# Router products between output tiles, expert 0 gathered before the full sort, and a software-pipelined expert loop

## What is computed

```python
x1 = layer_norm(ALPHA * x + mixer(x))                  # mixer: attention + retention, then @ w_out
# hierarchical MoE: top-1 of 4 groups, then top-2 of its 8 experts, 32 experts in all
g_logits = x1 @ w_group_router + b_group_router        # 4
e_logits = x1 @ w_expert_router + b_expert_router      # 4 x 8
g_sel = argmax(g_logits); top2 = top_k(e_logits[g_sel], 2)
weights = softmax(g_logits)[g_sel] * softmax(top2)
for e in experts:                                      # the rows of each expert
    hid = silu(rows @ w_gate[e]) * (rows @ w_up[e])    # 2048 -> 512
    y = hid @ w_down[e]                                # 512 -> 2048
x2 = layer_norm(ALPHA * x1 + sum over the token's two experts of weight * y)
```

## Time and profile before

| | us |
|---|---|
| median of three runs | 2180.9 (2179.12 to 2181.01) |
| the profiled execution, its own time | 2180.76 |
| its span | 2179.0 |
| PE busy | 2017.9 (93%) |
| DVE busy | 958.5 (44%) |
| ACT busy | 591.8 (27%) |
| POOL busy | 44.2 (2%) |
| mean granted TensorE clock | 0.948 |
| DMA, mean over the span | 283 GB/s |

### The profile page before, as it was taken

How to read it: one execution, slowest core, us unless ns; L and a number is a source line. 1 busy time by engine, 2 the same in 40 slices (tenths; PEclk the granted TensorE clock), 3 DMA queues, 4 the chain that set the end, 5 groups by cost and what they waited for, 6 DMA issues and landing times.

```text
span 2179.0 us, 23608 instructions
## 1 busy us (share of the span) xinstructions
PE 2017.9 (93%) x9124; PEld 1264.4 (58%) x9124; DVE 958.5 (44%) x1258; ACT 591.8 (27%) x736; POOL 44.2 (2%) x59
## 2 busy tenths in 40 slices
PE   9999999999999999999977988889888888998885
PEld 7888888888888888888855533333333333333331
DVE  5444554544444545565545433322333333233335
ACT  4444444334444344453423200000000000000000
POOL 0000000000000000000000000000000000000000
PEclk9999999999999999999989999999999989998997
DMA  7565455465555544566682599999999999999994
GB/s 237 183 200 177 155 168 169 156 202 173 193 184 164 174 159 161 182 229 228 204 313 76 209 429 428 428 428 428 428 429 429 429 429 428 428 429 429 428 429 174
DMA packets 147427, 617.01 MB, mean 283 GB/s; under 512 B 21024, under 2 KB 21152, under 8 KB 122272
## 3 DMA queue, kind: packets, MB, share of 16 engines
q1 hardware_dynamic: 147360, 616.09, 73.7%
HBM read 613.95 MB, written 2.10 MB: 283 GB/s over the span
## 4 chain that ended last, share of the span: by engine, by line
issue 57%; PE 35%; DVE 5%; ACT 2%; DVEq 0%; POOL 0%; POOLq 0%
PE PS L850 20%; PE PS L869 13%; DVE Z L1601 3%; PE PS L887 1%; DVE SG L1571 1%; PE PS L840 1%; ACT TG L1105 1%; PE PS L858 1%; ACT HT L1107 1%; POOL RSTD L1645 0%; PE PS L802 0%; ACT ZH L1085 0%; POOLq L1644 0%; DVE HB L1573 0%; PE PS L792 0%
## 5 line engine op out<-in xcount | busy, mean ns | idle before, releaser
L464 DVE TENSOR_TENSOR WL<-RAW,WH 128x1024 fp32r<-128x1024 f32 x384 | 457.6, 1221 | 394.7 <-ACT WH L460 393.8
L475 PE MATMUL PS<-WH,XH 128*128 128x512 f32 x1216 | 485.7, 399 | 4.6 <-DVE WL L464 3.4
L477 PE MATMUL PS<-WH,XL 128*128 128x512 f32 x1216 | 475.4, 391 | 0.0
L476 PE MATMUL PS<-WL,XH 128*128 128x512 f32 x1216 | 474.4, 390 | 0.0
L460 ACT ACTIVATE WH<-RAW 128x1024 fp32r<-128x1024 f32 x384 | 394.3, 1057 | 277.0 <-PE PS L477 223.2
L850 PE MATMUL PS<-W,XE 128*64 128x512 f32 x1984 | 430.9, 592 | 0.0
L850 PEld LDWEIGHTS PS<-W,XE 128*64 128x64 f32 x1984 | 139.3, 137 | 286.4 <-issue 286.4
L869 PE MATMUL PS<-W,HT 128*64 128x512 f32 x1024 | 290.8, 732 | 15.2 <-ACT HT L1107 15.2
L475 PEld LDWEIGHTS PS<-WH,XH 128*128 128x128 f32 x1216 | 228.9, 188 | 54.7 <-DVE WL L464 8.6
L477 PEld LDWEIGHTS PS<-WH,XL 128*128 128x128 f32 x1216 | 228.6, 188 | 49.2
L476 PEld LDWEIGHTS PS<-WL,XH 128*128 128x128 f32 x1216 | 229.0, 188 | 45.3
(11 more groups left out here) (262 smaller groups left out, 1360.8 us busy)
## 6 DMA issues: line engine op xcount, KB each, us to landing
RAW<-in_w_in_dram SPq DMA_DIRECT2D x304, 512.0 KB, 4.5
W<-in_w_expert_gate_dram SPq DMA_DIRECT2D x64, 2048.0 KB, 12.6
W<-in_w_expert_up_dram SPq DMA_DIRECT2D x64, 2048.0 KB, 17.0
W<-in_w_expert_down_dram SPq DMA_DIRECT2D x64, 2048.0 KB, 12.6
RAW<-in_w_branch_ret_dram SPq DMA_DIRECT2D x32, 512.0 KB, 4.8
RAW<-in_w_out_dram SPq DMA_DIRECT2D x32, 512.0 KB, 5.1
RAW<-in_w_branch_attn_dram SPq DMA_DIRECT2D x16, 512.0 KB, 4.6
XN<-in_x_dram SPq DMA_DIRECT2D x4, 512.0 KB, 8.2
```

Source lines behind the costliest of these rows:

```text
L464: dve.tensor_tensor(WL[:, i % RING], RAW[:, i % RING], WH[:, i % RING].bitcast(F32), ALU.subtract).then_inc(lo_done, 1)
L475: pe.matmul(PS[:, bank + t], hs, wh, start=first and j == 0, stop=False)
L476: pe.matmul(PS[:, bank + t], hs, wl, start=False, stop=False)
L477: mm = pe.matmul(PS[:, bank + t], ls, wh, start=False, stop=end)
```

## The change

Parts, in order of time:

1. **Router weights.** Loaded in the branch stage behind tiles 3 to 9, as 11 DMAs (runs of 64 and 128 bytes in the place of 16 and 32); DVE multiplies them by the norm's scale and bias behind branch tiles 18 to 23. The loads behind output tile 11 are gone but for RC.
2. **Logits from raw residual chunks.** Behind output tiles 10, 18 and 26 PE turns a chunk of un-normalised Z (8 turns), ACT copies it two tiles later, and behind tiles 14, 22 and 30 PE multiplies it by the weights (8 products 36 wide). The last chunk follows the last tile. Normalisation is put on the logits: LOG = logits * rstd + (NMR * column sums + bias).
3. **Norm and scaling.** ACT alone normalises Z and writes its high parts, reordered; POOL forms the low part of token tile 0, scales S1B and B1B, multiplies and adds them into Z (4 passes of 128x2048), clears the XT pad. DVE's four scaling passes are gone.
4. **Expert 0 first.** DVE builds SEL for the first 64 places, PE gathers 64 columns for 16 k (64 products 64 wide), ACT writes XE, `gate_up(0)` follows in one piece; the full sort of all 512 places comes after it.
5. **The expert loop** is pipelined: gate/up of expert i+2, turn and spread of earlier ones between its halves, down of i+1; slots of gate/up and down are freed by two counters; the last expert's down weights go into gate/up slots. The branch on `n_more` stands behind the last statistics on DVE.

```diff
+ROUTER_AT = (3, 4, 5, 6, 7, 8, 9)
+Z_TURN = {10: 0, 18: 1, 26: 2}
+Z_COPY = {n + 2: j for n, j in Z_TURN.items()}
+Z_LOGIT = {n + 4: j for n, j in Z_TURN.items()}
+CC_AT = 16
+FILL = 6
...
+        def load_router(m):
+            if m == 0:
+                sp.wait_ge(tile_used, T2 + RING)
+                sp.dma_start(WSG[:].rearrange("p j (b g) -> p j b g", b=4),
...
+            elif m <= NGRP:
+                g = m - 1
+                sp.dma_start(WST[:, :, g], w_expert_router[:, g].rearrange("l (j p b) e -> p (l j) (b e)", p=P, b=4),
...
-        with sp.Fori(1, NE) as e:
-            load_expert(e, e)
-        sp.wait_ge(xt_sums, KD)
+        load_gate_up(1, 1)
+        with sp.Fori(0, NE - 2) as i:
+            load_gate_up(i + 2, i + 2)
+            load_down(i + 1, i + 1)
+        load_last_down(NE - 1)
+        sp.wait_ge(scaled, TOK)
...
+        def turn_z(j, t):
+            for b in range(4):
+                mm = pe.transpose(PS[:, 6 + t, b * P:(b + 1) * P],
+                                  Z[:, t, j * CH:(j + 1) * CH].rearrange("p (c b) -> p b c", b=4)[:, b], rid)
+            mm.then_inc(zt_turned, 1)
+        def logits_of(j, t):
+            zt = ZT3[:, t] if j == 3 else ZTJ[t][:]
+            for b in range(4):
+                mm = pe.matmul(PS[:, 4 + t, 0:NR], zt[:, b * P:(b + 1) * P], WR[:, 4 * j + b],
+                               start=j == 0 and b == 0, stop=j == 3 and b == 3)
+            mm.then_inc(lg_sums, 1)
...
+        for k in range(KD):
+            gather_first(k)
+        for q in range(QS):
+            pe.wait_ge(xe_stored, KQ * (q + 1))
+            gate_up(0, q, XE)
+        for c in range(8):
+            sort_rows(2 * c)
+            sort_rows(2 * c + 1)
...
+        pe.wait_ge(table_ready, 1)
+        pe.wait_ge(h_ready, 1)
+        pe.wait_ge(xe_ready, 2)
+        gate_up(1, 0, XE)
+        turn_hidden(0)
+        gate_up(1, 1, XE)
+        down(0, range(KH), first=True)
+        with pe.Fori(0, NE - 2) as i:
+            pe.wait_ge(h_ready, i + 2)
+            pe.wait_ge(xe_ready, i + 3)
+            gate_up(i + 2, 0, XE)
+            turn_hidden(i + 1)
+            spread_rows(i, 0)
+            gate_up(i + 2, 1, XE)
+            spread_rows(i, 1)
+            down(i + 1, range(KH))
+        pe.wait_ge(h_ready, NE)
+        turn_hidden(NE - 1)
+        down(NE - 1, (0, 1), last=True)
+        spread_rows(NE - 2, 0)
+        down(NE - 1, (2,), last=True)
+        spread_rows(NE - 2, 1)
+        down(NE - 1, (3,), last=True)
...
+        for t in range(TOK):
+            act.activation(Z[:, t], Z[:, t], ACT.Identity, bias=NMR[:, t:t + 1],
+                           scale=RSTD1[:, t:t + 1]).then_inc(z_norm, 1)
+            act.wait_ge(z_norm, t + 1)
+            act.activation(ZHL[:, :, 0, t].rearrange("p (j k) c -> p j k c", j=QS), by_place(Z[:, t]),
+                           ACT.Copy).then_inc(z_high, 1)
...
+        dve.drain()
+        for t in range(TOK):
+            dve.scalar_tensor_tensor(LOGB[:, t], CC[:, 0], NMR[:, t:t + 1], CC[:, 1], ALU.mult, ALU.add)
+        dve.drain()
+        for t in range(TOK):
+            dve.wait_ge(lg_sums, 3 * TOK + t + 1)
+            dve.scalar_tensor_tensor(LOG[:, t], PS[:, 4 + t, 0:NR], RSTD1[:, t:t + 1], LOGB[:, t], ALU.mult, ALU.add)
...
-        low_half(1)
+        dve.wait_ge(z_high, 2)
+        dve.tensor_tensor(ZHL[:, :, 1, 1].rearrange("p (j k) c -> p j k c", j=QS), by_place(Z[:, 1]),
...
+        def select(cols):
+            iota = RC[:, R_IOTA + cols.start:R_IOTA + cols.stop]
+            for t in range(TOK):
+                dve.tensor_scalar(SELF[:, t, cols], iota, XPOS[:, 0, t:t + 1], None, ALU.is_equal)
+            dve.drain()
+            for t in range(TOK):
+                dve.scalar_tensor_tensor(SEL[:, t, cols], iota, XPOS[:, 1, t:t + 1], SELF[:, t, cols], ALU.is_equal,
+                                         ALU.add).then_inc(sel_ready, 1)
+        select(slice(0, ROWS))
...
+        select(slice(ROWS, ASSIGN))
-        for t in range(TOK):
-            dve.scalar_tensor_tensor(Z[:, t], Z[:, t], ALPHA, S1B[:], ALU.mult, ALU.mult)
...
+        pool.wait_ge(z_high, 1)
+        pool.tensor_tensor(ZHL[:, :, 1, 0].rearrange("p (j k) c -> p j k c", j=QS), by_place(Z[:, 0]),
+                           ZHL[:, :, 0, 0].rearrange("p (j k) c -> p j k c", j=QS).bitcast(F32),
+                           ALU.subtract).then_inc(z_low, 1)
+        pool.wait_ge(s1_landed, 32)
+        for v in (S1B, B1B):
+            pool.tensor_scalar(v[:], v[:], ALPHA, None, ALU.mult)
+        pool.wait_ge(z_low, 2)
+        pool.drain()
+        for t in range(TOK):
+            pool.tensor_tensor(Z[:, t], Z[:, t], S1B[:], ALU.mult)
+        pool.drain()
+        for t in range(TOK):
+            pool.tensor_tensor(Z[:, t], Z[:, t], B1B[:], ALU.add).then_inc(scaled, 1)
```

More of the change, by code:

```diff
@@ L861, in after_gate_up, with turn_hidden_more, down @@
             mm.then_inc(h_turned, 1)
-            pe.wait_ge(ht_ready, item + 1)
+        def turn_hidden_more(item):
+            pe.wait_ge(h_ready, item + 1)
             for b in range(KH):
+                mm = pe.matmul(PS[:, 1, b * ROWS:(b + 1) * ROWS],
+                               HB[0:ROWS].rearrange("p (c b) -> p b c", b=KH)[:, b],
+                               RC[0:ROWS, R_ID:R_ID + ROWS], start=True, stop=True)
+            mm.then_inc(h_turned, 1)
+        def down(item, blocks, first=False, last=False, more=False):
+            slot = 0 if last else GU
+            for b in blocks:
+                if b == 0:
+                    pe.wait_ge(ht_ready, item + 1)
+                    if not first:
+                        pe.wait_ge(y_dve, item * 2)
                 if b % KB2 == 0:
-                    pe.wait_ge(w_landed[GU + b // KB2], item * 16 + 16)
+                    pe.wait_ge(w_landed[slot + b // KB2], item * 16 + (32 if last else 0 if more else 16))
                 for n in range(2):
@@ L930, in _ @@
                 with pe.If(i < n_more):
-                    expert(i + NE)
-        spread_rows(n_more + (NE - 1))
+                    pe.wait_ge(xe_ready, i + (NE + 1))
+                    for q in range(QS):
+                        gate_up(i + NE, q, XE, more=True)
+                    turn_hidden_more(i + NE)
+                    down(i + NE, range(KH), more=True)
+                    for t in range(TOK):
+                        spread_rows(i + NE, t)
     @block.scalar
@@ L1357, in _ @@
                     residual(j)
-        residual(3)
+        dve.wait_ge(xc_landed, 16 * 4)
+        dve.wait_ge(tile_used, T4 + RING)
+        for t in range(TOK):
+            dve.scalar_tensor_tensor(Z[:, t, 3 * CH:D], XC[:, t], ALPHA, PS[:, out_pair(3) + t], ALU.mult,
+                                     ALU.add).then_inc(z3_done, 1)
+        dve.memset(NHF[:], -0.5)
         dve.drain()
-        dve.memset(NHF[:], -0.5)
+        for t in range(TOK):
+            dve.bn_stats(BS1[:, t, 3], Z[:, t, 3 * CH:D])
+        dve.drain()
         for t in range(TOK):
@@ L1619, in _ @@
             dve.bn_aggr(MV2[:, t], BS2[:, t].rearrange("p j s -> p (j s)")).then_inc(c_stats, 1)
+        dve.sem_inc(added, 2)
+        hidden(0)
+        hidden(1)
+        row_weights(0)
+        row_tokens(0)
+        with dve.Fori(0, NE - 2) as i:
+            y_low(i)
+            add_rows(i, 0)
+            hidden(i + 2)
+            row_weights(i + 1)
+            add_rows(i, 1)
+            row_tokens(i + 1)
+        y_low(NE - 2)
+        add_rows(NE - 2, 0)
+        row_weights(NE - 1)
+        add_rows(NE - 2, 1)
+        row_tokens(NE - 1)
+        y_low(NE - 1)
+        for t in range(TOK):
+            add_rows(NE - 1, t)
+            row_stats(t)
+        n_more = dve.value_load(ITAB[0:1, 2 * MORE:2 * MORE + 1], min_val=0, max_val=MORE)
+        with dve.If(n_more > 0):
+            with dve.Fori(0, MORE) as i:
+                with dve.If(i < n_more):
+                    hidden(i + NE)
+                    row_weights(i + NE)
+                    row_tokens(i + NE)
+                    y_low(i + NE)
+                    for t in range(TOK):
+                        add_rows(i + NE, t)
+            for t in range(TOK):
+                row_stats(t)
         dve.wait_ge(s2_landed, 32)
```

447 lines of the change are left out of this document (225 added, 222 removed).

## The result

The changed kernel takes 2193.79 us (median of 6 runs, 2189.61 to 2198.40) against 2179.34 us before (6 runs): a ratio of 1.0068, with a 95% interval of 1.0057 to 1.0079. That is 14.4 us slower, where 4.9 us faster was forecast, and it lies outside the range.

What follows compares the result with a forecast made beforehand. PE and DMA were taken as level, with the weight stream needing 29.3 us a round, so its start, early idling and end decide. Terms summed to -4.8 us from 2180.8, giving 2176 us; range 2158 to 2185.

Steps and rivals of the forecast that it cites:

- POOL ahead of SEL four times: Router, before SEL: a POOL pass gets in between each of DVE's four selection instructions; 2184 to 2193, 2188 us; chance 0.12.
- The forecast case: Router: DVE steps with two SBUF inputs wait out POOL passes, two of them behind CUM; 2176 us, spanning 2168 to 2183; 0.46.
- the sum: All terms against the profiled 2180.8 us: -6.9 - 0.3 - 4.3 + 10.8 - 4.8 + 0.7 = -4.8 us.
- The step that failed most: SEL: Last output product to SEL: LOG comes 15.5 us earlier, but DVE's waits for POOL take it back; -0.3 us.
- Output stage: XC issued earlier cuts PE's stall by 14.8 us, while added turns, products and column sums cost time; -6.9 us.
- Gather: Ahead of gate/up(0): 64 products 64 wide, 8.5 us in all, replace 40 products 512 wide lasting 12.8; -4.3 us.
- DMA idle: Near the stream's start: slots for expert 2 wait for the full sort and gate/up(1), DMA idles 16.0 us; +10.8 us.
- Loop and end: Expert rounds stay 29.3 us, bound by DMA; down(31) ends 10.6 us after the last weights, not 15.4; -4.8 us.

Runs made afterwards that it cites:

- the ladder: Follow-up runs ordered from the kernel before to the changed kernel, adding parts step by step: 2179.4, 2167.1, 2165.1, 2164.9, 2175.5, 2193.8 us.

## Why the prediction was wrong

**Which case came.** By its deciding point it was the rival "POOL ahead of SEL four times", with 2188 us and 0.12: SEL ready more than 38 us after the last output product; it was ready 39.0 us after it. The forecast case differed from it by how many passes get in between. But three passes were waited out behind CUM, two of them over Z, not four, and the measured 2193.8 us lies 0.8 above that rival's upper end, since other terms failed with it. The profile is 22.3 us above the sum: 7.6 by SEL, 7.0 by the gather and gate/up behind it, 4.4 by the output stage, 3.3 by the rest.

**The step that failed most: SEL.** Forecast -0.3, measured +7.3 (gather start against last product, 31.8 to 39.1). That DVE's steps wait for POOL's passes was right, though no row had shown it in this direction. The count and the sizes were wrong. A scaling was put at 2.1 us from POOL's copy and takes 5.37, as long as the low part (5.52, put at 4.2); the Z passes take 4.5 each (put at 4.2). The Trainium skill (GPSIMD Engine Reference, section 3.1, Elementwise — side-by-side cycle accounting) states 4497 ns for an fp32 `tensor_tensor` addition of 2048; the trace agrees, with 4496 ns for the product of Z and S1B and 4526 to 4680 for the additions of B1B. As to the count, SELF waited out one pass, but SEL of both token tiles waited one each, and my sum had one for both. Up to CUM the sizes hid each other: +8.5 us against +8.2, but by luck, since the low part held DVE for 5.3 us (put at 4.0) and of the two scalings only one stood in its way before CUM, for 3.5 us (the two put at 4.2). All of the loss lies between CUM and SEL, +14.0 against +7.0: one pass more than counted (4.5 us), a reordered low part on DVE of 3.94 us where 2.28 was taken, and 4.3 us of the second scaling ahead of SELF where 3.6 of a Z pass were taken.

**Output stage.** Forecast -6.9, measured -2.5. The cause was right, as the run with the loads alone shows (-12.3), but the stall fell to 3.3, not to 0.3, and the work put between the tiles costs 3.6 us for turns and 5.6 for products, 9.2 us, where the sum had 7.9. Behind the last product the 15 us that LOG gains are then spent: with nothing in the way PE starts the sort 23 us after that product (32 before), a gain of 9 us for which 9.2 were paid between the tiles. This part of the change is a draw (-2.0 us in the ladder).

**Gather.** Forecast -4.3, measured +0.6, and 2.1 more in gate/up(0). The term that failed is the 64 x 0.13 us of the sum: no row has the 0.13, and 64 x 0.13 leaves hardly any of the 5 us that the text allows for a slow start. The pitch is 0.21 us at a granted clock of 0.50, and 0.10 at 1.00; the clock stayed at 0.50 through all 64. The row that the text names, 0.20 us, would have given 12.8 us, near the measured 13.4, though by luck: it is two records of 0.10 us at a clock of 1.00.

**DMA idle.** Forecast +10.8, measured +9.9 by the windows with all small gaps counted (8.6 to 18.5 us), +11.5 with the loop; the hole alone grew from 5.0 to 16.7 us (5.2 and 16.0 in the sum). This step was right, and it decides against the gather: with its cause isolated the order costs 10.7 us.

**Loop and end.** Rounds of 29.3 us and DMA as the bound: right (29.41). The gain at the end, -4.8, came as -3.6 in the profile but not in the time, since the rounds got 0.17 us longer. The prediction had PE and the stream level; what it did not draw from it is that anything added to either then shows in full: 0.2 us on PE's side in the old loop, the new order of loads on the stream's. "By itself it gives nothing" was right.

**The chances.** The forecast case had 0.46 though its two POOL durations stood on one row with another operation, and its count of passes on nothing. The argument against the rival, that DVE issues its pairs without a wait between them, held for the two SELF, which waited once (4.56 us together), and not for the two SEL (4.5 us each). With the four passes at 2184 to 2193 and their weight at 0.12 the range ended where that case began.

## What to carry to other kernels

Before work goes to POOL, look at what DVE does in the same microseconds: a short DVE step on the critical path with two SBUF inputs, or a `tensor_scalar`, can cost a whole POOL pass, and the next one waits right behind. Then look at what is queued behind the pass on POOL itself.

Try each part of a large change alone. Here five parts were one edit, the best of them was the moving of some small DMAs (12.3 us), and two others cost 29 us; none of this could be seen from their sum.

In a loop that is level with its DMA, a wait that is always satisfied is not free on the engine whose chain makes the round: taking it out, 0.2 us at its place, gave 11.5 us over 31 experts.

## What the hardware showed that I had not expected

- POOL's scaling of one row set (one tensor input, a constant) takes 5.37 us for 128x2048, against 4.5 us for a product of two tensors and 1.05 us for a copy of 1024.
- A `tensor_scalar` of 64 columns waits for POOL as a two-input operation does (two take 4.56 us, 0.42 without POOL), a reduction between two such waits does not (0.29 us). Beside a scaling the two-input step gets through some 1.9 us ahead of the end of POOL's record (LATER 3.68 us of 5.37), the `tensor_scalar` does not (5.13 and 1.54 us in the kernel before with two scalings added).
- The wait works against POOL too: 8.29 us for a pass of 5.37 when DVE's step of 3.94 us was under way (8.26 to 8.30 in three runs).
- TensorE's clock fell from 1.00 to 0.50 while PE was busy with narrow products back to back (64 columns, each with its own stationary tile), after it had been 1.00 during wide ones. Filling the wait ahead of them did not keep it.
